# Expert layout of a two-layer diffusion trunk on one core: ten blocks with parts of 32, 64 or 128 slots, a seventh weight buffer, and a later start of the result gathers

## The chip, the core and the metric

The kernel runs on one core of one Trainium2 chip. The metric is the device time of one launch in microseconds; less is better. TensorE does the matrix products, VectorE and ScalarE copy and combine, GpSimd computes small scalars and issues the indexed transfers, and SyncE issues the weight transfers. All transfers run on the core's 16 DMA engines.

## The reference

One inference step of a trunk with two layers over 384 tokens (128 context, 256 latent) of width 1024. Each layer has a mixer (windowed attention beside a state-space scan) and then a mixture of 16 experts of which each token uses two. The mixture is what the change touches:

```
def moe_ffn(h, w_router, router_bias, w_gate_l, w_up_l, w_down_l):
    ...
    scores = jax.nn.sigmoid((t @ w_router).astype(jnp.float32))
    sel = scores + router_bias.astype(jnp.float32)
    grp = sel.reshape(-1, N_EXPERT_GROUPS, EXPERTS_PER_GROUP)
    grp_score = lax.top_k(grp, TOP_K)[0].sum(axis=-1)
    best = jnp.argmax(grp_score, axis=-1)
    ...
    _, idx = lax.top_k(masked, TOP_K)
    ...
    hid = jax.nn.silu(jnp.einsum('nd,edf->enf', t, w_gate_l)) * jnp.einsum('nd,edf->enf', t, w_up_l)
    hid = hid * gates.T[:, :, None].astype(hid.dtype)
    out = jnp.einsum('enf,efd->nd', hid, w_down_l)
```

Everything is float32. An expert has three matrices of 1 MB (gate, up: 1024 x 256; down: 256 x 1024), so a layer's experts are 48 MB of weights. Worked out from the reference's router on its inputs, the tokens of experts 0 to 15 are 38, 35, 30, 51, 43, 30, 42, 31, 99, 72, 105, 52, 45, 13, 45, 37 in layer 0 and 57, 50, 46, 37, 21, 24, 31, 26, 48, 76, 62, 38, 69, 49, 47, 87 in layer 1.

## The kernel before

The program is written by hand for the five engines, each with its own sequence and explicit waits on semaphores; no scheduler moves anything. The mixture of one layer runs so:

- Routing. TensorE makes router scores, VectorE chooses two experts a token, TensorE sums their positions. `FIXED` experts (0 and 1) have slots whatever their load. The other experts are ranked by their number of tokens; the ranking (`order`, L1442, signalled by `s_order`) tells SyncE which expert's weights to load next.
- Blocks. The work is cut into `NB` = 11 blocks of 128 slots. A block is a full expert (128 slots) or two experts of 64 slots: experts 0 and 1 and the ranks 0 to 3 have a block each, the ten lighter experts share five. For a block VectorE builds a one-hot selection (`fixed_one_hot`, `one_hots`), TensorE turns it into token numbers (`slot_tokens`, in four lists, `LISTS`), VectorE writes `idx`, and GpSimd gathers the token rows from `h_rows` (L711). TensorE transposes the rows (`rows`, L2218), multiplies by gate and up (`gate_up`, L2228, 8 steps), transposes the hidden values (L2235) and multiplies by down (`down`, L2244, 4 steps). Two 64-slot halves are products of 64 stationary columns each, issued in turn into the two halves of one bank. The sequence is `first_half(b+1)`, `hid_of(b)`, `rows(b+2)`, `second_half(b)`. `rows(1)` and the third list stand in the middle of `first_half(0)`.
- Results. ScalarE copies a block's result (`store`, L997) and, for the first `STORED` = 8 blocks, stores it in `y_exp` (L1002). The last three blocks (`LATE`) stay on chip and are added by products with a selection (`late_results`, L2290). For the stored ones GpSimd gathers, per token tile t of three, two result rows per token (L718, 0.5 MB each, six gathers) once the blocks' stores have landed; ScalarE scales the one (`weighted`, L1007), VectorE adds the other (L1550), then come gate and residual (`added`, `late_added`, `updated`) and the next layer's norm.
- Weights. SyncE loads units of 2 MB (gate and up of one expert, or down of a pair) into `ring`, six buffers (`SLOTS`). Each unit waits until its buffer's last holder has been used (`EARLIER`). Three mixture units (experts 0 and 1) can be loaded before the ranking is known, the others only after it. After the mixture of layer 0, SyncE waits for the last result gather (`combined`) before it loads the next layer's input weights.
- `clock_kept` is products that compute nothing and keep TensorE at work while it has to wait.

`xn` (3 x 1024 per partition) holds the normed tokens, then the accumulated results (`acc`); `xpad` (3072) holds the convolution input, then gates and gathered results (`first_y`).

## Time and profile before

| | us |
|---|---|
| median of 3 runs | 799.59 |
| lowest, highest | 797.41, 799.68 |
| profiled execution, whole | 799.34 |
| its span | 797.6 |
| TensorE busy in the span | 742.6 (93%) |
| VectorE, ScalarE, GpSimd busy | 329.5, 216.4, 142.0 |
| moved by DMA | 211.56 MB, mean 265 GB/s |

The span is the profiled execution without 1.7 us around it. In the trace the mixture of layer 0 lies between about 250 and 412 us, that of layer 1 between about 625 us and the end. TensorE's busy time counts overlapping products once. A row of a timeline names its idle time before it, and who ended it, in brackets.

### The profile page before, as it was taken

The numbers are of one execution on the slowest core, as the hardware profiler recorded it, in microseconds if no ns is written. First come the engines' busy times: TensorE is split into PE (matmuls) and PEld (weight loads), VectorE is DVE, ScalarE is ACT, GpSimd is POOL, SyncE is SP. The second block draws the span as 40 slices with busy tenths as digits, with TensorE's granted clock in tenths as the row PEclk, the third lists the DMA queues.
The fourth block names the chain that finished last, engine by engine and source line by source line (L and its number), as shares of the span: only waits on it lengthen the run. The fifth ranks groups of instructions, "written<-read, shape, count | busy, mean of one in ns | idle before, by whom it ended". The sixth has DMA issues, their size and how long they took to land. (4 is left out here: it accounts for less than half of the span.)

```text
span 797.6 us, 9586 instructions
## 1 busy us (share of the span) xinstructions
PE 742.6 (93%) x3528; PEld 372.2 (47%) x3528; DVE 329.5 (41%) x874; ACT 216.4 (27%) x492; POOL 142.0 (18%) x238
## 2 busy tenths in 40 slices
PE   3999997999999999999999999889999799999994
PEld 1456652455446444443344755345545544444331
DVE  2023534656436453212272262564643734331136
ACT  2210255724023110111312025683312301101121
POOL 4146041120011200000212404222000120000202
PEclk9999998999999999999999999999999999999998
DMA  8997225679422999999897233657420499999961
GB/s 323 387 341 252 95 107 211 219 283 400 181 74 114 390 392 409 424 424 422 315 389 246 83 106 112 212 176 295 190 106 1 158 409 357 418 424 421 424 241 79
DMA packets 66340, 211.56 MB, mean 265 GB/s; under 512 B 7883, under 2 KB 8755, under 8 KB 54003
## 3 DMA queue, kind: packets, MB, share of 16 engines
q1 hardware_dynamic: 52744, 179.33, 58.1%
q10 hardware_dynamic: 7851, 17.70, 5.8%
q0 software_dynamic: 5696, 13.89, 4.9%
q8 instruction: 29, 0.48, 0.2%
q14 instruction: 20, 0.16, 0.1%
HBM read 202.02 MB, written 13.93 MB: 271 GB/s over the span
## 5 line engine op out<-in xcount | busy, mean ns | idle before, releaser
L2228 PE MATMUL bank<-ring,work 128*64 128x512 f32 (+1 forms) x512 | 157.6, 598 | 3.0 <-DMA ring<-in_w_up_dram 2.5
L2228 PEld LDWEIGHTS bank<-ring,work 128*64 128x64 f32 (+1 forms) x512 | 59.1, 158 | 96.0 <-issue 94.4
L2244 PE MATMUL bank<-ring,xs_tok 128*64 128x512 f32 (+1 forms) x256 | 79.9, 597 | 2.0 <-DVE xs_tok L1573 1.0
L1573 DVE COPY xs_tok<-bank 128x256 f32<-128x256 f32 x22 | 9.3, 424 | 149.2 <-PE bank L2235 149.2
L1858 PE MATMUL bank<-hT,ring 128*128 128x384 f32 x192 | 62.2, 486 | 0.0
L1732 PE MATMUL bank<-ring,cpad 128*32 128x512 f32 x384 | 49.4, 636 | 6.6 <-DMA ring<-in_w_ada_dram 5.8
L1858 PEld LDWEIGHTS bank<-hT,ring 128*128 128x128 f32 x192 | 36.5, 190 | 25.0
L2244 PEld LDWEIGHTS bank<-ring,xs_tok 128*64 128x64 f32 (+1 forms) x256 | 28.3, 157 | 39.1 <-issue 35.0
L990 ACT ACTIVATE xs_tok<-bank 128x256 f32<-128x256 f32 x22 | 8.5, 385 | 139.7 <-PE bank L2228 139.7
L2116 PE MATMUL bank<-ring,xn 128*128 128x512 f32 x96 | 43.6, 597 | 0.0
L997 ACT ACTIVATE qkv<-bank 128x512 f32<-128x512 f32 x40 | 21.7, 595 | 79.4 <-PE bank L2244 79.4
L2116 PE MATMUL bank<-ring,xs_tok 128*128 128x512 f32 x96 | 43.2, 592 | 0.0
L1803 PE MATMUL bank<-ring,hT 128*128 128x512 f32 x96 | 42.8, 597 | 0.4 <-ACT hT L801 0.4
L1915 PE MATMUL bank<-ring,hT 128*128 128x512 f32 x96 | 42.3, 593 | 0.0
L711 POOL DMA_INDIRECT hT<-h_rows,idx x18 | 18.4, 1022 | 126.7 <-PE bank L2218 77.7
L1562 DVE COPY work<-bank 128x512 f32<-128x512 f32 x42 | 27.1, 686 | 11.6 <-PE bank L2218 11.6
L1170 DVE SCALAR_TENSOR_TENSOR conv<-xpad,prm,conv 128x388 f32<-128x388 f32 x48 | 29.9, 623 | 1.7
L2116 PEld LDWEIGHTS bank<-ring,xs_tok 128*128 128x128 f32 x96 | 18.2, 190 | 23.0 <-issue 23.0
L1803 PEld LDWEIGHTS bank<-ring,hT 128*128 128x128 f32 x96 | 17.7, 190 | 22.6 <-issue 20.4
L1915 PEld LDWEIGHTS bank<-ring,hT 128*128 128x128 f32 x96 | 17.8, 190 | 20.1 <-issue 20.1
L2116 PEld LDWEIGHTS bank<-ring,xn 128*128 128x128 f32 x96 | 17.4, 190 | 19.2 <-issue 19.2
L1732 PEld LDWEIGHTS bank<-ring,cpad 128*32 128x32 f32 x384 | 10.6, 113 | 29.1 <-issue 20.6
(392 smaller groups left out, 1057.2 us busy)
## 6 DMA issues: line engine op xcount, KB each, us to landing
ring<-in_w_ada_dram SPq DMA_DIRECT2D x48, 1024.0 KB, 8.8
ring<-in_w_gate_dram SPq DMA_DIRECT2D x32, 1024.0 KB, 13.1
ring<-in_w_up_dram SPq DMA_DIRECT2D x32, 1024.0 KB, 16.8
ring<-in_w_down_dram SPq DMA_DIRECT2D x32, 1024.0 KB, 14.6
ring<-in_w_in_dram SPq DMA_DIRECT2D x16, 1024.0 KB, 14.5
ring<-in_w_out_dram SPq DMA_DIRECT2D x8, 1024.0 KB, 7.3
y_exp<-qkv ACTq DMA_DIRECT2D x16, 512.0 KB, 8.4
xpad<-gate_rows ACTq DMA_DIRECT2D x6, 512.0 KB, 4.9
```

The costliest lines, as they stand in the source:

```text
L711: pool.indirect_dma_start(out=xg[b % 4], out_offset=None, in_=h_rows[:, :], in_offset=bass.IndirectOffsetOnAxis(ap=idx[:, b:b + 1], axis=0 ...
L997: act.activation(y_buf(e)[:, hf * 512:(hf + 1) * 512], bank[5 + hf][:, :], ACT.Copy).then_inc(s_yc, 1)
L1170: ins = dve.scalar_tensor_tensor(out=conv[:, m, :], in0=xpd[:, m, k:k + CONVW], scalar=tap(k), in1=conv[:, m, :], op0=ALU.mult, op1=ALU.add)
L1562: dve.tensor_copy(xgT[:, b, hf * 512:(hf + 1) * 512], bank[3 + hf][:, :]).then_inc(s_xgc, 1)
L1573: dve.tensor_copy(hidT[:, b, :], bank[2][:, 0:F]).then_inc(s_htc, 1)
L1732: last = mm(bank_of(i)[ADA_TILE * q:ADA_TILE * (q + 1), :], cpad[:, c:c + ADA_TILE], slot(ADA_AT[j])[:, kt, :], start=j == a and kt < ADA_ ...
L1803: last = mm(bank[t][:, :], tok(kt, t), slot(u[0])[:, kt, :], start=kt == 0, stop=kt == KT - 1)
L1858: last = mm(bank[(6 + m) % 8][:, 0:3 * P], slot(v)[:, kt, col:col + P], hT[:, kt, :], start=kt == 0, stop=kt == KT - 1)
L1915: last = mm(bank[4 + t][:, :], tok(kt, t), slot(u[3])[:, kt, :], start=kt == 0, stop=kt == KT - 1)
L2116: last = mm(bank[2 * t + hf][:, :], mixed[:, t, kt * P:(kt + 1) * P] if kt < 4 else xs_tok[:, t, (kt - 4) * P:(kt - 3) * P], slot(u + hf)[ ...
L2228: last = mm(bank[b][i * n:(i + 1) * n, :].rearrange("p (i f) -> p i f", i=2), rows_T[:, kt * P + i * n:kt * P + (i + 1) * n], gate_up_of(s ...
L2244: last = mm(bank[5 + hf][i * n:(i + 1) * n, :], hidT[:, b, f * P + i * n:f * P + (i + 1) * n], w[:, f, hf * 512:(hf + 1) * 512], start=f = ...
```

## The change

The layout has ten blocks instead of eleven:

- Experts 0, 1 and 2 are fixed, with 96 slots each. Of the 13 ranked ones, ranks 0 and 1 have 128 slots, ranks 2 and 3 have 96, ranks 4 to 11 have 64, and rank 12 has 32. Together these are 1280.
- A block holds parts of one width: one of 128, two of 64, or four of 32. An expert of 96 slots is three parts of 32, or one of 32 and one of 64 in another block. Three blocks a layer (0, 2 and 5) have four parts, five have two, two have one. Expert 2 lies in blocks 1 and 2, so its weights stay until block 2 has used them.
- `STORED` is 7; results are stored at rows of their expert, in one or two transfers a block, 12 a layer instead of 8 (of 3.7 MB instead of 4.2 MB).
- `xn` and `xpad` become one tensor, `arena`, and 4096 columns in it are a seventh buffer (`EXTRA`), which holds rank 0's and then another expert's gate and up. The results are gathered over the same columns.
- Four and a half units instead of three can be loaded before the ranking: gate and up of 0, 1 and 2, down of 0 and 1, down of 2.
- The second list of slots (block 1) moves behind the ranking on VectorE, and behind the other products on TensorE.
- GpSimd waits for the layer's last weight unit before it issues the six result gathers, and ScalarE scales all three tiles after its last `store`, not between the stores; VectorE adds tile 0 after the loop.
- The landing semaphores are counted over seven, and two semaphores for norm weights become one.
- VectorE computes the new capacities with six small operations more, in `combination`.

```
-FIXED = 2
+FIXED = 3
-SLOTS = 6
+SLOTS, EXTRA, LANDED = 6, 6, 7
...
+FULL, WIDE, NARROW = 2, 4, 12
+FIXED_CAP = 96
+cap_of = lambda r: CAP if r < FULL else HALF + CAP // 4 if r < WIDE else HALF if r < NARROW else CAP // 4
...
+quarters = lambda x, *at: tuple((x, Q * i, Q) for i in at)
+BLOCKS = [parts_of(*quarters(0, 0, 1, 2), *quarters(1, 0)),
+          parts_of((1, Q, HALF), (2, 0, HALF)),
+          parts_of(*quarters(2, 2), *quarters(3, 0, 1, 2)),
+          parts_of((4, 0, CAP)),
+          parts_of((5, 0, CAP)),
+          parts_of(*quarters(6, 0, 1, 2), *quarters(7, 0))] + [parts_of((x, 0, HALF), (x + 1, 0, HALF)) for x in (8, 10, 12, 14)]
...
+        extra = arena[:, DM:DM + UNIT]
...
-        LISTS = ((0, 1), (1, 2), (2, 7), (7, NB))
-        ROWS_AT = 5
+        LISTS = ((0, 1), (1, 2), (2, 6), (6, NB))
+        ROWS_AT = 4
...
+                    if EARLIER[u] is not None:
+                        sp.wait_ge(*used(EARLIER[u]))
+                    else:
+                        sp.wait_ge(s_h, 16 * NT * (l + 1))
+                        sp.wait_ge(s_x1, 2 * NT * (l + 1))
...
+                u = MOE_AT[l] + MOE_U - 1
+                pool.wait_ge(landed[u % LANDED], 32 * (u // LANDED + 1))
                 pool.wait_ge(s_yidx, l + 1)
...
-                    if e == NB - 2:
-                        act.wait_ge(s_yidx, l + 1)
-                        weighted(0)
-                    if e == NB - 1:
-                        weighted(1)
-                        weighted(2)
...
                     store(e, e % 2)
+                act.wait_ge(s_yidx, l + 1)
+                for t in range(NT):
+                    weighted(t)
...
                 lists(0)
-                lists(1)
-                clock_kept(4, 4)
+                clock_kept(4, 6)
                 if l == 0:
                     ada_columns(ADA_GAP)
-                clock_kept(4, 4)
+                clock_kept(4, 2)
+                lists(1)
...
-                        for i, s in enumerate(slots):
-                            last = mm(bank[b][i * n:(i + 1) * n, :].rearrange("p (i f) -> p i f", i=2),
-                                      rows_T[:, kt * P + i * n:kt * P + (i + 1) * n], gate_up_of(s)[:, kt, :, :],
+                        for s, at, n in parts:
+                            last = mm(bank[b][at:at + n, :].rearrange("p (i f) -> p i f", i=2),
+                                      rows_T[:, kt * P + at:kt * P + at + n], gate_up_of(s)[:, kt, :, :],
                                       start=kt == 0, stop=kt == KT - 1)
```

TensorE's sequence from the first list of layer 0 to block 1's first products. `tok_id` products are the lists (one bank each), `amask` products are `clock_kept`, `ident,hT` products transpose gathered rows, `ring,work` products are gate and up. Before:

```order
L1755 MATMUL bank4<-amask,ident 128x256 x2
L2195 MATMUL bank3<-tok_id,conv 128x2 x3
L2195 MATMUL bank0<-tok_id,conv 128x2 x3
L1755 MATMUL bank4<-amask,ident 128x256 x4
L1748 MATMUL bank5<-fold,qkv 128x4 x4
L1755 MATMUL bank4<-amask,ident 128x256 x4
L2218 MATMUL bank3<-ident,hT 128x128 x4
L2218 MATMUL bank4<-ident,hT 128x128 x4
L1755 MATMUL bank2<-amask,ident 128x256
L2228 MATMUL bank0<-ring,work 128x512 x4
L2218 MATMUL bank3<-ident,hT 128x128 x4
L2218 MATMUL bank4<-ident,hT 128x128 x4
```

And now:

```order
L2280 MATMUL bank3<-tok_id,conv 128x2 x3
L1840 MATMUL bank4<-amask,ident 128x256 x6
L1833 MATMUL bank5<-fold,qkv 128x4 x4
L1840 MATMUL bank4<-amask,ident 128x256 x2
L2280 MATMUL bank0<-tok_id,conv 128x2 x3
L2303 MATMUL bank3<-ident,hT 128x128 x4
L2303 MATMUL bank4<-ident,hT 128x128 x4
L1840 MATMUL bank2<-amask,ident 128x256
L2312 MATMUL bank0<-ring,work 32x512 x16
L2303 MATMUL bank3<-ident,hT 128x128 x4
L2303 MATMUL bank4<-ident,hT 128x128 x4
L2280 MATMUL bank2<-tok_id,conv 128x2 x12
```

The second list (bank0) now stands last before block 0's rows are transposed, and block 0's products are in sets of four with 32 columns each.

SyncE's weight issues around the wait for the ranking (`expert_order_made`) in layer 0. Before:

```order
L464 DMA ring<-in_w_down_dram 128x2048 [waits out_mm]
L464 DMA ring<-in_w_down_dram 128x2048
L514 TENSOR_LOAD qT [waits expert_order_made]
L514 ISA x2
L464 ISA [waits out_mm]
L464 DMA ring<-in_w_gate_dram 128x2048
L464 DMA ring<-in_w_up_dram 128x2048
L514 TENSOR_LOAD qT
L514 ISA x2
L464 ISA [waits ada_mm]
L464 DMA ring<-in_w_gate_dram 128x2048
L464 DMA ring<-in_w_up_dram 128x2048
```

And now:

```order
L533 DMA ring<-in_w_gate_dram 128x2048 [waits out_mm]
L533 DMA ring<-in_w_up_dram 128x2048
L533 DMA ring<-in_w_down_dram 128x2048 [waits out_mm]
L533 DMA ring<-in_w_down_dram 128x2048
L533 DMA ring<-in_w_down_dram 128x2048 [waits ada_mm]
L582 TENSOR_LOAD qT [waits expert_order_made]
L582 ISA x2
L533 ISA [waits ada_mm]
L533 DMA ring<-in_w_gate_dram 128x2048
L533 DMA ring<-in_w_up_dram 128x2048
L533 DMA ring<-in_w_down_dram 128x2048
L582 TENSOR_LOAD qT
```

The gate and up of expert 2 and one half of the split down unit now stand ahead of the wait, 3 MB more; behind it comes the other half (the row with one down issue), and next, not shown, the seventh buffer's unit.

GpSimd's gathers of rows (`h_rows`) and of results (`y_exp`) in layer 0. Before:

```order
L711 DMA hT<-h_rows,idx 128x1024 [waits xg_transposed,slot_tokens_made] x3
L711 DMA rot<-h_rows,idx 128x1024 [waits xg_transposed,slot_tokens_made]
L711 DMA hT<-h_rows,idx 128x1024 [waits xg_transposed,slot_tokens_made] x3
L718 DMA rot<-y_exp,y_idx 128x1024 [waits y_stored0,y_stored1,result_rows_made,xg_transposed]
L718 DMA xn<-y_exp,y_idx 128x1024
L718 DMA xpad<-y_exp,y_idx 128x1024
L718 DMA xn<-y_exp,y_idx 128x1024
L718 DMA xpad<-y_exp,y_idx 128x1024
```

And now:

```order
L792 DMA rot<-h_rows,idx 128x1024 [waits slot_tokens_made]
L792 DMA hT<-h_rows,idx 128x1024 [waits xg_transposed,slot_tokens_made] x3
L792 DMA rot<-h_rows,idx 128x1024 [waits xg_transposed,slot_tokens_made]
L792 DMA hT<-h_rows,idx 128x1024 [waits xg_transposed,slot_tokens_made] x2
L799 DMA rot<-y_exp,y_idx 128x1024 [waits y_stored0,result_rows_made,y_stored1,landed3,xg_transposed]
L799 DMA arena<-y_exp,y_idx 128x1024 x5
```

The first of them also waits for `landed3`, the semaphore of the last unit.

## Rows read from the trace of the kernel before

**Rows 1.** Stretches: start:end, length, busy us by engine (count), PEclk, DMA, GB/s.

```profile
320.00:360.00 40.00, 40.00 (x168) 17.32 (x166) 8.80 (x25) 4.58 (x10) 0.99 (x1) 1.00 1.01 423
600.00:640.00 40.00, 35.16 (x196) 22.14 (x195) 22.21 (x63) 11.69 (x27) 4.13 (x7) 0.96 0.26 100
720.00:760.00 40.00, 39.37 (x167) 16.16 (x167) 6.12 (x12) 4.41 (x9) 5.94 (x6) 1.00 1.01 422
```

**Rows 2.** TensorE timeline (start us, us, line, operands): expert blocks, `clock_kept` at 629.54.

```profile
284.14 7.09 PE L2228 MATMUL bank<-ring,work 128*64 128x512 f32 x32
...
295.74 7.03 PE L2228 MATMUL bank<-ring,work 128*128 128x512 f32 x16
...
379.89 7.09 PE L2228 MATMUL bank<-ring,work 128*64 128x512 f32 x32 [1.90 <-DMA ring<-in_w_up_dram]
...
629.54 3.70 PE L1755 MATMUL bank<-amask,ident 128*128 128x256 f32 x16
...
659.71 7.09 PE L2228 MATMUL bank<-ring,work 128*64 128x512 f32 x32
...
767.98 3.65 PE L2244 MATMUL bank<-ring,xs_tok 128*64 128x512 f32 x16 [0.94 <-DMA ring<-in_w_down_dram]
```

**Rows 3.** TensorE timeline: two sets of four 32-wide products, and what follows them.

```profile
20.88 1.92 PE L1732 MATMUL bank<-ring,cpad 128*32 128x512 f32 x16
22.73 0.70 PE L1755 MATMUL bank<-amask,ident 128*128 128x256 f32 x2
```

**Rows 4.** SyncE timeline, layer 0: issues before and after the ranking.

```profile
234.15 0.80 SPq L464 DMA_DIRECT2D ring<-in_w_down_dram  x2
259.17 0.36 SPq L464 DMA_DIRECT2D ring<-in_w_gate_dram  x1
```

**Rows 5.** TensorE timeline, layer 0: selection sums, row transposes, first products.

```profile
254.84 0.21 PE L2195 MATMUL bank<-tok_id,conv 128*128 128x2 bf16 x3
...
258.00 1.97 PE L1755 MATMUL bank<-amask,ident 128*128 128x256 f32 x8
261.05 1.06 PE L2218 MATMUL bank<-ident,hT 128*128 128x128 f32 x8 [1.08 <-DMA hT<-h_rows,idx]
...
262.97 3.70 PE L2228 MATMUL bank<-ring,work 128*128 128x512 f32 x8 [0.42 <-DVE work L1562]
266.82 1.09 PE L2218 MATMUL bank<-ident,hT 128*128 128x128 f32 x8 [0.15 <-DMA hT<-h_rows,idx]
```

**Rows 6.** GpSimd timeline, layer 0: gathers of token rows for blocks 0 and 1.

```profile
257.03 1.18 POOL L711 DMA_INDIRECT hT<-h_rows,idx  x1 [12.78 <-DVE idx L1412]
258.52 1.05 POOL L711 DMA_INDIRECT hT<-h_rows,idx  x1 [0.30 <-issue]
```

**Rows 7.** The chain that ended last, layer 1: start us, us, what.

```profile
632.59 10.37 DMA hT<-h_rows,idx
...
742.86 7.80 DMA y_exp<-qkv
...
757.98 14.36 DMA xn<-y_exp,y_idx
```

**Rows 8.** ScalarE, then TensorE timeline, end of layer 0.

```profile
395.31 1.15 ACT L1007 ACTIVATE xn<-xn,wt 128x1024 f32<-128x1024 f32 x1 [0.73 <-DMA xn<-y_exp,y_idx]
...
396.33 2.84 PE L2290 MATMUL bank<-qkv,conv 128*128 128x512 f32 x6
...
405.88 1.88 PE L2290 MATMUL bank<-qkv,conv 128*128 128x512 f32 x4
408.63 1.09 PE L1774 MATMUL bank<-ident,xn 128*128 128x128 f32 x8 [0.87 <-DVE xn L1118]
```

**Rows 9.** TensorE where its clock was low: timeline, then busy time by stretch.

```profile
637.80 4.74 PE L2228 MATMUL bank<-ring,work 128*128 128x512 f32 x8
...
136.00:139.00 3.00, 2.95 (x14) 0.96 (x18) 0.62 (x3) 3.00 (x11) 0.67 (x2) 0.50 0.02 7
790.00:797.00 7.00, 0.00 (x0) 0.00 (x0) 2.91 (x3) 1.15 (x2) 0.73 (x2) 0.51 0.39 156
```

257 lines of the change are left out of this document (152 added, 105 removed).

## The prediction

> **What bounds the kernel now.** I first read the busy time by stretch [rows 1]. TensorE has no gap to speak of, so that view alone would make a dropped block worth its whole time. But in the two stretches inside the mixtures the DMA engines are full as well, at 422 to 423 GB/s, while just before the mixture of layer 1 they are used to 26%. The TensorE timeline [rows 2] shows which of the two is behind: the last block waits 1.90 us for gate and up weights in layer 0, and in layer 1 the last down product waits until 767.98. Transfers and products end together. The chain of waits [rows 7] says what the end really follows: a block's result lands at 750.66, the six result gathers are issued, the last at 757.98, and they land at 772.34, far behind because weights flow beside them. In layer 0 the last one lands at 395.31 [rows 8]. So the bound of each mixture is the stream of weights and gathers, and the price of the change is what it does to the landing of the last result rows: 395.31 and 772.34.
>
> **One block fewer.** A block is 11.6 us of TensorE: one gate and up starts at 284.14, the next at 295.74 [rows 2]. That is off the path except where it frees buffers, and the transfers shrink by one row gather and half a megabyte of stores, 1 MB a layer, 2.5 us of stream.
>
> **Four parts a block.** Two sets of four 32-wide products take 22.73 - 20.88 = 1.85 us to the next product, 0.93 a set [rows 3]; a step of two 64-wide ones takes 0.88 (eight in 7.0 us, [rows 2]). So I take 0.05 a step, 12 steps a block, 0.6 us a block with four parts, and 1.8 us a layer for three. The bounds are 0 and 0.12 a step. The Trainium skill, "TensorE: Matmul & The Clock Gate", Part 3 on packing small matmuls, measured a speedup of 2.38, not 3, for three column tiles of 32; at that rate a set of four takes 1.1 us, and the sum below would be 6 us longer. The rows show four packing almost fully.
>
> **More weights ahead of the ranking.** Before, the last unit that needs no ranking is issued at 234.15 and the next at 259.17 [rows 4], in a time when the DMA engines are mostly idle. Now 3 MB more land there, worth 3.15 / 0.423 = 7.4 us of stream, in a time when no one waits. The seventh buffer takes 2 MB more right after the ranking. But the gain is not kept, because buffers then run out. The two gate and up units of block 5 get the buffers of experts 2 and 3, which come free only when block 2's gate and up is done, since expert 2 lies in blocks 1 and 2, and SyncE issues in order. By a count of the units in that order everything issued until then (4.2 MB behind block 0's and 1's gate and up) has landed some 5 us before. So the stream rests, restarts there, and is full to the end.
>
> **The second list moved back.** Before, block 1's rows are gathered from 258.52, right behind block 0's [rows 6], and TensorE transposes them at 266.82 after 0.15 us of waiting [rows 5]. Now their list stands behind all clock-keeping products, which end at 258.00 + 1.97 = 259.97 [rows 5]. From block 0's list at 254.84 [rows 5] to its gather at 257.03 [rows 6] were 2.2 us with ranking work between; without that I take 1.6 us, so the gather starts at about 261.3 (the list itself may be 0.3 earlier, since VectorE builds one selection before it, not two). That is 2.8 us later, and `first_half(0)` has `rows(1)` in its middle: TensorE stops there until 269.6. In layer 1 the gather before starts at 632.59 and takes 10.37 us [rows 7]; there the keeping products end at 629.54 + 3.70 = 633.24 [rows 2], and the gather starts 1.9 us later, so its rows land at 644.9. Bounds are 0 (the DMA engines give the late gather a larger share) and 5 us (it queues behind the weights issued first). Behind this wait stand lists 2 and 3 and all later gathers, so the whole block sequence shifts with it.
>
> **When block 2's gate and up ends.** Before, with `rows(1)` at 266.82, it ends at 291.1 [rows 2], 24.3 us later. Now 0.8 us of four-part steps come in and 0.4 us of a small row wait goes: 269.6 + 24.7 = 294.3. In layer 1: 643.0 to 666.7 [rows 2, 7] is 23.7; 644.9 + 24.5 = 669.4.
>
> **The stream after it.** 15 units of 2.097 MB, six stores and four row gathers of 0.524 MB are 36.7 MB. At 423 GB/s [rows 1] that is 86.8 us: the last weights land at 381.1 in layer 0. In layer 1, at 422, at 756.4, and 0.4 more for the final norm's weights, which ScalarE now loads beside it: 756.8. In layer 1 before it was 767.98.
>
> **The result gathers.** Before, the last of six is issued 757.98 - 750.66 = 7.3 us after its release [rows 7]. Now it is released by the last weights. Alone, a gather takes 261.05 - 257.03 = 4.0 us from issue to use [rows 5, 6], not 14.36. So the last result rows land 11.3 us after the last weights: 392.4 and 768.1, that is 2.9 and 4.2 us earlier than before. The Trainium skill, "DMA: Bandwidth & Descriptors", fits a transfer issued by GpSimd as 2.0 us plus its bytes at 436 GB/s; that would be 3.2 us, and 0.8 us a layer better. On GpSimd nothing is queued behind the new wait but the norm. SyncE waits for the gathers before it loads the next layer's input weights; these have 15 us until they are needed at about 410.
>
> **Behind the gathers.** TensorE's last block ends, before, at 396.33 [rows 8]. Now: -11.6 -1.9 (the weight wait) +2.8 +1.8 = 387.4. ScalarE's copies and three scalings follow, and the third has to wait for 392.4 anyway: moving `weighted` behind the stores costs nothing unless the rows come before 390. The late products, 11.4 us without a wait (396.33 to 407.76), are over at 398.9. The next layer's transposes, before at 408.63, hang on VectorE's chain and come at 405.7. So TensorE stands still for 6.8 us where it stood 0.87. What the clock does after such a rest: in the last 7 us, without a product, it is granted at 0.51, the 1.2 GHz level [rows 9]. Back at work it stays there for a while: eight products took 4.74 us instead of 3.70, a loss of 1.0 [rows 9, 5], and in 136 to 139 the clock is 0.50 with TensorE busy all the time, a loss of 1.5 in that stretch alone. TensorE is the bound from the transposes on, so this counts. I take 2.1, between 1.0 and twice 1.5. In layer 1 nothing follows that needs the clock.
>
> **The six small VectorE operations** and the extra store issues lie beside products; VectorE is busy 8.8 of 40 us there [rows 1]. Without that cover they would be some 1 us a layer.
>
> **Sum.** -2.9 (layer 0) + 2.1 (clock) - 4.2 (layer 1) = -5.0 us. 799.34 - 5.0 = 794.3; the median shown is 0.25 above the profiled execution, so I forecast **794.5**. Its own range is 791 to 798.
>
> **Rivals.**
>
> *The stream does not rest.* If block 1's rows come without the delay, or the early 3 MB carry through, the last weights land by 376 and 751, and TensorE sets the end: its last block at 387.4, in layer 1 at 762.8 (771.6 - 11.6 - 0.9 + 1.9 + 1.8), then 1.1 us of copies and three scalings of 1.15. The last scaling starts at 390.8 and 766.2: 4.5 and 6.1 us gained, 2.1 given back, 791. For it: 7.4 us of prefetch. Against it: the buffers. 17%.
>
> *Parts of 32 do not pack.* A set of four takes 0.93 us if all run at once and 2 x 0.88 if two do. At 1.1, 20 sets before block 2's gate and up is done cost 0.17 each more, 3.4 us a layer, and the time is 801, within 0.3% of before. Against it: [rows 3]. The skill's figure above is this case. 6%.
>
> *The stop in `first_half(0)` becomes the bound, slower.* TensorE stops there in a place where it already rested for the first rows. If block 1's gather takes 2 us more than before, and the clock falls in the stop, as it did in layer 1 (4.74 for 3.70), another 2.1 us, every later buffer is freed 4 us later, and so are the last weights: 8.4 us in all, 802.7. It decides from the point where block 2's gate and up ends 2.9 us after 294.3 in layer 0 and 4.2 us after 669.4 in layer 1; from there nothing is gained. For it: DMA is full from 259, and the early issues stand ahead of that gather. Against it: before, the same gather shared the engines with as many weights. 14%.
>
> *The layout does not hold the tokens.* Then an overflow round runs all 16 experts again, 50 MB or 119 us of stream at 423 GB/s: over 900 us. Loads by rank are 105, 99, 72, 52, 51, ... 13 and 87, 76, 69, 62, 49, ... 21, against 128, 128, 96, 96, 64, ... 32; fixed ones at most 57 of 96. Excluded but for an error: 1%.
>
> **How the numbers follow.** The forecast has 55%. Small mixtures around no change have 7%. A measurement of this kernel tells 0.3%, 2.4 us, from no change. Faster: 51 of the forecast's 55 and the 17 of the first rival, 68%. Within: 4, the 6, the 7 and 2 of the slower rival, 19%. Slower: 13%. The range goes from 3 below the first rival to the middle between the second and the third: 788 to 801.5; about 1 in 10 lies outside on either side.
>
> **What would show it.** Right: the transposes of block 1's rows wait 2 to 3 us; DMA falls for some 5 us before block 2's gate and up ends, and is full from then on; the last down weights land near 381 and (shifted by layer 0) 756; the last result gather needs about 4 us; TensorE rests 5 to 8 us before the next layer's transposes and runs at half clock after it. Wrong: TensorE's blocks waiting for weights from block 3 on (stream slower than taken), or the last scaling following ScalarE's copies at once (the first rival), or four-part blocks over 8 us of gate and up.

## The result: slower, and the profile of the changed kernel

The changed kernel takes 806.68 us (median of 20 runs), the kernel before 799.92 in the same comparison. The ratio is 1.0074, with a 95% interval of 1.0058 to 1.0090: 0.74% slower. Two of the 20 executions, of 969.52 and 1262.68 us at granted clocks of 0.75 and 0.56, are slow ones that the ratio leaves out. Forecast were 794.5, with a range of 788 to 801.5. The profiled execution has a span of 806.8 us where it was 797.6.

Five marks that both programs have show where the 9.2 us came from.

| | before | after | step after | difference of the step |
|---|---|---|---|---|
| layer 0: last down product ends | 396.40 | 398.55 | | +2.15 |
| first transposes of the next norm | 408.63 | 415.76 | 12.23, now 17.21 | +4.98 |
| layer 1: routing sums begin | 627.61 | 637.73 | 218.98, now 221.97 | +2.99 |
| last down product ends | 771.63 | 778.18 | 144.02, now 140.45 | -3.57 |
| end of the span | 797.6 | 806.8 | 25.97, now 28.62 | +2.65 |

Only one step is shorter. With one block of 11.6 us fewer, the mixture of layer 0 still ends 2.15 us later, and what follows each mixture is longer.

**The head of layer 0.** The row transposes of block 0, which stood at 261.05 with 1.08 us of waiting [rows 5], in TensorE's timeline of the changed kernel:

```profile
266.68 1.94 PE L2303 MATMUL bank<-ident,hT 128*128 128x128 f32 x8 [6.62 <-DMA hT<-h_rows,idx]
...
291.31 7.05 PE L2312 MATMUL bank<-ring,work 128*32 128x512 f32 x64
```

The gather they wait for, in GpSimd's timeline, and the first weights behind the ranking in SyncE's:

```profile
257.94 1.29 POOL L792 DMA_INDIRECT hT<-h_rows,idx  x1 [13.26 <-DMA h_rows<-arena]
```

```profile
258.64 0.35 SPq L533 DMA_DIRECT2D ring<-in_w_gate_dram  x1
```

Before, the gather was issued at 257.03, as soon as its list was there [rows 6], 2.1 us ahead of the first weights at 259.17 [rows 4]. Now it waits for something else, the landing of the last `h_rows` store, and starts at 257.94, 0.9 us later, while the first weights go 0.5 us earlier, at 258.64. The lead is down to 0.7 us. Its rows come 8.7 us after the issue instead of 4.0.

Stretches of the same kernel (start:end, length, busy us by engine and count, PEclk, DMA, GB/s):

```profile
245.00:250.00 5.00, 4.07 (x58) 2.76 (x51) 3.72 (x12) 2.68 (x8) 0.00 (x0) 1.00 1.00 362
250.00:255.00 5.00, 4.55 (x42) 2.60 (x40) 4.18 (x18) 2.79 (x6) 0.00 (x0) 1.00 0.95 384
260.00:265.00 5.00, 0.05 (x3) 0.00 (x0) 2.02 (x6) 0.00 (x0) 1.01 (x1) 0.66 0.95 382
265.00:270.00 5.00, 3.33 (x14) 2.31 (x18) 1.28 (x3) 1.33 (x2) 0.00 (x0) 0.50 1.02 424
275.00:280.00 5.00, 5.00 (x53) 1.77 (x53) 4.12 (x17) 0.00 (x0) 2.67 (x3) 1.00 0.28 66
295.00:300.00 5.00, 5.00 (x44) 2.06 (x38) 2.96 (x15) 0.38 (x1) 0.00 (x0) 1.00 0.64 212
```

In the first two stretches the DMA engines are full with the weights loaded ahead of the ranking; the `h_rows` stores, issued at 246.5, 251.4 and 252.9, go through the same engines. Before, the DMA share there was 0.27 and 0.53. From 260 to 265 TensorE does next to nothing (0.05 us), and its granted clock falls to 0.66 and then to 0.50, the 1.2 GHz level: the transposes take 1.94 us instead of 1.06. Then comes what the forecast had named, a pause of the stream: 66 GB/s from 275 to 280 and 212 from 295 to 300, since buffers come free late.

**The tail of layer 0.** TensorE, GpSimd, ScalarE (with its last scaling of layer 1) and VectorE, from the last block on:

```profile
363.59 7.09 PE L2312 MATMUL bank<-ring,work 128*64 128x512 f32 x32 [1.14 <-DMA ring<-in_w_up_dram]
...
379.70 9.44 PE L2312 MATMUL bank<-ring,work 128*64 128x512 f32 x32 [4.20 <-DMA ring<-in_w_up_dram]
...
394.90 3.65 PE L2327 MATMUL bank<-ring,xs_tok 128*64 128x512 f32 x16
...
415.76 1.97 PE L1859 MATMUL bank<-ident,arena 128*128 128x128 f32 x8 [5.85 <-DVE arena L1199]
```

```profile
390.26 0.99 POOL L799 DMA_INDIRECT rot<-y_exp,y_idx  x1 [65.37 <-DMA ring<-in_w_down_dram]
...
396.75 0.99 POOL L799 DMA_INDIRECT arena<-y_exp,y_idx  x1 [0.30 <-issue]
```

```profile
398.88 1.08 ACT L1080 ACTIVATE work<-bank 128x512 f32<-128x512 f32 x2 [4.08 <-PE bank L2327]
399.85 3.22 ACT L1091 ACTIVATE arena<-arena,wt 128x1024 f32<-128x1024 f32 x3
```

```profile
781.56 1.15 ACT L1091 ACTIVATE arena<-arena,wt 128x1024 f32<-128x1024 f32 x1 [0.18 <-DMA arena<-y_exp,y_idx]
```

```profile
401.03 1.29 DVE L1636 SCALAR_TENSOR_TENSOR arena<-rot,wt,arena 128x1024 f32<-128x1024 f32 x1 [6.53 <-ACT arena L1091]
402.36 2.61 DVE L1636 SCALAR_TENSOR_TENSOR arena<-arena,wt 128x1024 f32<-128x1024 f32 x2
405.00 1.22 DVE L1641 TENSOR_TENSOR arena<-arena,conv 128x1024 f32<-128x1024 f32 x1
```

The last block waits 4.20 us for gate and up weights, and its eight steps take 9.44 us where they took 7.09 [rows 2]. The last down product starts at 394.90, the copies at 398.88, and the three scalings follow without a wait. The result rows, gathered from 390.26 on, are there at 401.65, where SyncE, which waits for them, issues again; the third scaling starts at about 402.0. So two things end together behind the last block: TensorE with ScalarE's copies and scalings, and the rows, which waited for the last weights. In layer 1 it is the rows: the third scaling, at 781.56 (shown among the rows above), waits 0.18 us for them. VectorE begins the last addition of its chain (L1641) at 405.00, 6.5 us after the end of TensorE's last down product (394.90 + 3.65); before it did so (L1555) at 397.87, 1.5 us after it. These are the 5.0 us of the table. TensorE then stands still for 5.85 us, and its clock is low again.

The end of the stream, the same columns as above:

```profile
384.00:386.00 2.00, 2.00 (x12) 0.77 (x10) 0.00 (x0) 0.00 (x0) 0.00 (x0) 0.88 1.01 422
386.00:388.00 2.00, 2.00 (x12) 0.73 (x10) 0.00 (x0) 0.00 (x0) 0.00 (x0) 1.00 0.37 152
388.00:390.00 2.00, 1.50 (x8) 0.35 (x4) 0.46 (x2) 0.39 (x1) 0.00 (x0) 1.00 0.04 16
390.00:396.00 6.00, 5.98 (x26) 2.11 (x28) 0.71 (x2) 1.09 (x2) 4.52 (x5) 1.00 0.55 160
396.00:402.00 6.00, 6.00 (x20) 2.32 (x17) 0.97 (x1) 3.12 (x5) 1.44 (x2) 1.00 0.62 213
```

The weights flow at 422 GB/s until 386.3, and the last of them lands near 389: two and a half us with 0.3 MB in them. The gathers, which wait for it, then have the DMA engines alone and move 160 and 213 GB/s.

### The profile page after: what moved, and what is told of

Same layout as the page of the kernel before. It is cut to its first block and busy times, and to the rows that moved or that the text cites. A ratio compares the mean times of both kernels' runs of the same rounds, so it can differ in the third digit from the quotient of the medians.

```text
span 806.8 us, 10286 instructions
## 1 busy us (share of the span) xinstructions
PE 730.4 (91%) x3886; PEld 356.5 (44%) x3886; DVE 325.0 (40%) x882; ACT 213.1 (26%) x486; POOL 141.4 (18%) x234
## 5 line engine op out<-in xcount | busy, mean ns | idle before, releaser
L2312 PE MATMUL bank<-ring,work 128*32 128x512 f32 (+2 forms) x704 | 134.1, 619 | 10.3 <-DMA ring<-in_w_up_dram 9.9
L2312 PEld LDWEIGHTS bank<-ring,work 128*32 128x32 f32 (+2 forms) x704 | 42.1, 129 | 97.0 <-issue 95.4
L2327 PE MATMUL bank<-ring,xs_tok 128*32 128x512 f32 (+2 forms) x384 | 73.0, 597 | 1.0 <-DVE xs_tok L1659 1.0
L2201 PE MATMUL bank<-ring,arena 128*128 128x512 f32 x96 | 43.6, 597 | 0.0
L1080 ACT ACTIVATE qkv<-bank 128x512 f32<-128x512 f32 x36 | 19.5, 595 | 79.3 <-PE bank L2327 79.3
L2327 PEld LDWEIGHTS bank<-ring,xs_tok 128*32 128x32 f32 (+2 forms) x384 | 22.4, 127 | 38.4 <-issue 35.3
L1648 DVE COPY work<-bank 128x512 f32<-128x512 f32 x38 | 24.6, 686 | 15.0 <-PE bank L2303 15.0
L1251 DVE SCALAR_TENSOR_TENSOR conv<-arena,prm,conv 128x388 f32<-128x388 f32 x48 | 29.9, 623 | 1.7
L2303 PE MATMUL bank<-ident,hT 128*128 128x128 f32 x128 | 18.3, 291 | 11.9 <-DMA hT<-h_rows,idx 11.9
L2312 PE MATMUL bank<-arena,work 128*128 128x512 f32 (+1 forms) x64 | 28.4, 597 | 0.0
```

The costliest lines, as they stand in the source:

```text
L1080: act.activation(y_buf(e)[:, hf * 512:(hf + 1) * 512], bank[5 + hf][:, :], ACT.Copy).then_inc(s_yc, 1)
L1251: ins = dve.scalar_tensor_tensor(out=conv[:, m, :], in0=xpd[:, m, k:k + CONVW], scalar=tap(k), in1=conv[:, m, :], op0=ALU.mult, op1=ALU.add)
L1648: dve.tensor_copy(xgT[:, b, hf * 512:(hf + 1) * 512], bank[3 + hf][:, :]).then_inc(s_xgc, 1)
L2201: last = mm(bank[2 * t + hf][:, :], mixed[:, t, kt * P:(kt + 1) * P] if kt < 4 else xs_tok[:, t, (kt - 4) * P:(kt - 3) * P], slot(u + hf)[ ...
L2303: last = tr(bank[3 + kt // 4][:, kt % 4 * P:(kt % 4 + 1) * P], buf[:, kt * P:(kt + 1) * P], ident[:, :])
L2312: last = mm(bank[b][at:at + n, :].rearrange("p (i f) -> p i f", i=2), rows_T[:, kt * P + at:kt * P + at + n], gate_up_of(s)[:, kt, :, :], ...
```

## Experiments

My theory after this reading had two parts. **The head**: weights issued behind the ranking overtake block 0's rows. **The tail**: the scalings stand behind the last store and lengthen the chain behind the last block. The rivals: the amount of the stream decides whatever is done at either end, or the new wait of GpSimd is the loss. All ratios are against the kernel before, run on the same chip; the x, y and z runs were on three chips, so runs of different letters are compared by their ratios.

| kernel | what differs | median us | ratio | 95% interval |
|---|---|---|---|---|
| changed kernel |  | 806.68 | 1.0074 | 1.0058 to 1.0090 |
| x1_rows0 | SyncE waits for block 0's rows | 798.25 | 0.9964 | 0.9942 to 0.9986 |
| x2_rows01 | and for block 1's | 800.24 | 0.9994 | 0.9978 to 1.0010 |
| x3_list1 | second list as before | 798.37 | 0.9981 | 0.9960 to 1.0001 |
| x4_nolast | no wait for the last weights | 809.29 | 1.0080 | 1.0051 to 1.0109 |
| y1_results | that, and the scalings as before | 795.21 | 0.9907 | 0.9875 to 0.9939 |
| y2_layout | that, and the second list as before | 789.07 | 0.9842 | 0.9805 to 0.9878 |
| y3_before_late | kernel before, scalings behind, last-weights wait | 813.49 | 1.0155 | 1.0129 to 1.0180 |
| z4_before_behind | kernel before, scalings behind | 813.13 | 1.0149 | 1.0128 to 1.0171 |
| y4_keep | y2_layout, 16 keeping products | 790.07 | 0.9857 | 0.9834 to 0.9881 |
| z1_ordered | y2_layout, SyncE waits for block 0's rows | 786.47 | 0.9827 | 0.9807 to 0.9847 |
| z2_ordered_keep | z1_ordered, 16 keeping products | 789.54 | 0.9851 | 0.9829 to 0.9872 |
| z3_six | z1_ordered, no seventh buffer | 795.21 | 0.9926 | 0.9905 to 0.9948 |

### The head: the gather alone (x1_rows0, x2_rows01)

```
                     if (pair, k) == (SPLIT[0], 1):
                         sp.wait_ge(s_order, l + 1)
+                        sp.wait_ge(gathered[0], 16 * (uses(BUFS, 0) * l + 1))
```

The second run has the same line for `gathered[1]` as well.

> The changed kernel, but SyncE waits, behind the ranking, until block 0's token rows have landed before it issues further weights. Theory 'the head': in the changed kernel the first rows land at 266.7 (261.05 before) because weights issued at 258.6 flow beside their gather; alone it needs 4 us, so rows(0) comes at about 262.3 in layer 0, the clock does not fall to 0.50, the first products take 3.7 and not 4.8 us, and block 2's gate and up ends at 293 to 295 instead of 298.3. Since the stream rests until then, the later issue of the weights costs nothing, and the last weights land 3 to 4 us earlier a layer: 799 to 802 us against 806.7. Rival 'the stream': the amount of weights behind sets the end, the later issue only delays it; the last weights stay at 389 or come later, 806 to 809 us.

> As the run with SyncE waiting for block 0's rows, but it waits for block 1's rows too. Theory 'the head': block 1's gather is alone as well and takes 4 us instead of 8 to 10; in layer 0 it was in time behind the late first rows, in layer 1 TensorE waited 2.90 us for it. So rows(1) comes at about 266 in layer 0, and block 2's gate and up ends at about 292; weights that block 2 needs at 285 are issued at about 266, in time. 797 to 801 us. If the weights behind the ranking are needed sooner than that, TensorE waits for them in block 2 and the time is that of the changed kernel, 805 to 808 us.

The first run is 1.1% faster than the changed kernel by the ratios, 8.8 us, a little more than expected: the head's theory holds and the rival falls. TensorE's row transposes in it, and the last block:

```profile
262.86 1.94 PE L2304 MATMUL bank<-ident,hT 128*128 128x128 f32 x8 [1.75 <-DMA hT<-h_rows,idx]
...
373.91 9.39 PE L2313 MATMUL bank<-ring,work 128*64 128x512 f32 x32 [4.20 <-DMA ring<-in_w_up_dram]
```

The rows come 4.0 us after the issue at 258.87, as before the change, and the last block starts 5.8 us earlier. It still waits 4.20 us for weights, so the stream bounds it in this run too; what moved is the whole sequence. The line acts in both layers. By the marks of the table above, 5.8 of the 10.5 us between the two profiled executions come in the mixture of layer 0 and 4.5 in that of layer 1. There block 0's rows had hardly been late (4.6 us after their issue, here 4.2). Block 1's had: TensorE waited 2.90 us for them in the changed kernel, and here it does not wait at all. Their gather is now issued ahead of the weights (638.23 against 639.70) and not behind them (644.24 against 642.24).

The second run's time lies in its range, but it gains nothing on the first, and block 1's rows come at 270.57, not at 266. They had not been late in layer 0, and SyncE now issues its first weights 2.0 us later (265.8 instead of 263.8). The last block starts 2.3 us later, at 376.2. Of these, 1.2 us are not the weights': block 0's first products, whose weights were loaded long before, took 5.02 us in this execution where they took 3.76 in the first run. The intervals of the two ratios overlap a little, so what the later issue itself costs is not shown; that it is worth something to wait for the second gather too is not shown either.

### The list's place (x3_list1)

On VectorE `one_hots(0, LISTS[1][1])` builds both selections first, and `slot_tokens(1)` and `lists(1)` stand where they stood before the change.

```
                 lists(0)
+                lists(1)
                 clock_kept(4, 6)
...
                 clock_kept(4, 2)
-                lists(1)
```

> The changed kernel with the second list of slots where it was before: ahead of the ranking on VectorE and right behind the first list on TensorE. Theory 'the head': SyncE's issues come about 0.5 us later as before, both gathers are issued at about 258 and 259.5 and share the engines with the weights; the first rows still land late (263 to 266), so at most 1 to 2 us a layer come back: 803 to 806 us. Rival 'the list': the later list is the whole loss, and the time falls to 799 or below.

The rival's number came, 798.4, not mine. But not by the rival's mechanism:

```profile
257.20 1.23 POOL L792 DMA_INDIRECT hT<-h_rows,idx  x1 [13.01 <-DVE idx L1493]
258.73 1.01 POOL L792 DMA_INDIRECT hT<-h_rows,idx  x1 [0.30 <-issue]
```

```profile
258.94 0.35 SPq L533 DMA_DIRECT2D ring<-in_w_gate_dram  x1
```

```profile
261.45 1.06 PE L2302 MATMUL bank<-ident,hT 128*128 128x128 f32 x8 [1.40 <-DMA hT<-h_rows,idx]
...
267.38 1.09 PE L2302 MATMUL bank<-ident,hT 128*128 128x128 f32 x8 [0.38 <-DMA hT<-h_rows,idx]
```

Block 0's gather is issued 1.7 us ahead of the weights, and its rows land in time, at 261.45, with 1.40 us of waiting. The list's place moved the weights 0.3 us back, and in this execution the gather was free to go when its list was there, 0.7 us earlier; that was enough. The list of block 1 itself was never late in layer 0. In layer 1 it was: by the marks this execution is 8.3 us ahead of the changed kernel's at the end of layer 0's mixture and gains another 4.1 in that of layer 1, where block 1's rows are there in time (642.58, no wait). That a shift of some tenths decides was the question of a later run (z1_ordered).

### The wait for the last weights (x4_nolast), and the results as before (y1_results)

```
-                u = MOE_AT[l] + MOE_U - 1
-                pool.wait_ge(landed[u % LANDED], 32 * (u // LANDED + 1))
                 pool.wait_ge(s_yidx, l + 1)
```

> The changed kernel without GpSimd's wait for the last weights: the six result gathers are issued once the stored blocks have landed, at about 370, and flow beside the last weights. If the wait costs (the gathers, 3.15 MB or 7.4 us of stream, end 12.3 us behind the last weights, at 401.65, and the last scaling with them), the rows are there when the last block's copies are done at 400 and 1 to 2 us a layer come back, unless the last weights land up to 7.4 us later. If the wait gains, as its place says, the last block waits for its weights up to 7 us longer (4.2 us now) and the time rises to 809 to 815 us. I expect slightly slower, 807 to 812.

y1_results has this and ScalarE's and VectorE's old order too:

```
+                    if e == NB - 2:
+                        act.wait_ge(s_yidx, l + 1)
+                        weighted(0)
+                    if e == NB - 1:
+                        weighted(1)
+                        weighted(2)
...
                     store(e, e % 2)
-                act.wait_ge(s_yidx, l + 1)
-                for t in range(NT):
-                    weighted(t)
```

> The changed kernel with its part on the results undone: no wait for the last weights on GpSimd, and the three scalings between the last stores. Theory 'the tail': from the last down product's end to the next layer's transposes are 17.3 us in the changed kernel (398.5 to 415.8) and 12.3 before (396.4 to 408.6); to the end of the span they are 28.6 and 26.0, because three scalings and VectorE's first additions stand behind the last copies. Without the last-weights wait alone nothing came back (809.3 against 806.7), since the scalings still stood there. Undone together they give 5.0 + 2.6 = 7.6 us: 799 to 802 us. Rival 'only the head and the weights count': the time stays at 805 to 809.

Without the wait the ratio is 1.0080, with it 1.0074: as long as the scalings stand behind the last store, the wait of GpSimd neither costs nor gains. The gathers issued at 372.1 delay the last block's weights by little (it starts at 379.05, with 4.82 us of waiting), and the rows are there by 393.87, 7.8 us sooner than with the wait, for scalings that start at 398.27.

With the wait gone, the order of the scalings (and of VectorE's first addition) does cost: x4_nolast and y1_results differ in nothing else, and lie 1.7% apart.

The other single edit, the old order with the wait kept, was not run. From the rows of the changed kernel my estimate is that it would give back 1 us at most: from the landing of the last rows (401.65, 781.56) to VectorE's L1641 (405.00, 784.34) are 3.35 and 2.78 us, where the kernel before has 2.56 and 2.55 (395.31 to 397.87, 772.37 to 774.92). So by the rows either part is enough to hold the chain back, and only undoing both frees it.

The profiled spans of x4_nolast and y1_results are 807.3 and 793.5. By the marks of the table above, the 13.8 us are 2.7 up to the last down product of layer 0 (block 0's rows came that much earlier in this execution of y1_results), 5.6 from there to the next transposes (16.92 and 11.29), 1.4 to the routing of layer 1, -0.2 in its mixture and 4.2 behind it (28.6 and 24.4). So the scalings' place costs 11.2 us here. I had expected 799 to 802 us from the two edits, a gain of 7.6; the median is 795.21, since with the rows in time both chains get shorter than they were in the kernel before.

### The same two edits on the kernel before (y3_before_late, z4_before_behind)

Both put the scalings behind the last store of the kernel before; y3_before_late also adds the wait for the last weights.

> The kernel before with the change's part on the results alone: GpSimd waits for the layer's last weights, and the scalings stand behind the last store. Forecast of the blind sum: the gathers land 11 to 12 us behind the last weights. Before, those flow beside the gathers until about 390 and 767; without them the last weights come up to 7.4 us (3.15 MB) sooner, about 384 and 760. Theory 'the tail': the last scaling then follows at about 400 (396.4 + 1.0 + 3.2) instead of 396.5 and the next transposes at 413 instead of 408.6: 2 to 4 us a layer lost, 803 to 808 us. Rival 'the earlier weights pay for it': 797 to 801.

> The kernel before with the three scalings behind the last store (and VectorE's first addition behind the loop), but no wait for the last weights. It splits the 12 us that both together cost the kernel before (813.5 against 801.6). From the traces: scalings behind the last copies put 5.0 us between the last down product and the next transposes of layer 0 and 2.6 us behind layer 1, and the clock falls in that rest (1 to 2 us): 808 to 811 us. What is left to 813.5 is the wait's: rows that land at 402.2 and 786.3 where the copies end at 398 and 781.5. If the wait were the whole, the time would stay at 801 to 803.

1.0155 with both, 1.0149 with the scalings alone: on this kernel too the order of three ScalarE instructions (with VectorE's first addition) is enough for the whole loss, 12 us, and the wait adds nothing that can be measured on top. Both expectations were too small, the first by 5 us and the second by 2. The rival of the first (earlier weights pay) fell: the last weights land at about 390 without the gathers beside them. That does not clear the wait. In y3_before_late ScalarE does wait for the late rows, in both layers:

```profile
402.19 1.15 ACT L1009 ACTIVATE xn<-xn,wt 128x1024 f32<-128x1024 f32 x1 [0.82 <-DMA xn<-y_exp,y_idx]
...
786.33 1.15 ACT L1009 ACTIVATE xn<-xn,wt 128x1024 f32<-128x1024 f32 x1 [1.37 <-DMA xn<-y_exp,y_idx]
```

By the marks, its steps behind the two last blocks are 1.7 and 2.1 us longer than those of z4_before_behind, and the mixtures ahead of them 1.4 and 2.4 us shorter. The wait alone on this kernel was not run. ScalarE, VectorE and TensorE of z4_before_behind:

```profile
399.32 3.22 ACT L1007 ACTIVATE xn<-xn,wt 128x1024 f32<-128x1024 f32 x3
```

```profile
400.51 1.28 DVE L1547 SCALAR_TENSOR_TENSOR xn<-rot,wt,xn 128x1024 f32<-128x1024 f32 x1 [6.25 <-ACT xn L1007]
```

```profile
380.11 8.78 PE L2224 MATMUL bank<-ring,work 128*64 128x512 f32 x32 [2.13 <-DMA ring<-in_w_up_dram]
...
415.24 1.97 PE L1770 MATMUL bank<-ident,xn 128*128 128x128 f32 x8 [5.57 <-DVE xn L1115]
417.00 3.62 PE L2286 MATMUL bank<-qkv,conv 128*128 128x512 f32 x4
```

By the marks of the table above, its 13.8 us over the span before are: 1.9 up to the last down product (394.66 + 3.65), 4.7 to the next transposes, 2.9 to the routing of layer 1 (637.12), 1.4 to the last down product of layer 1 (782.56), 2.9 to the end. The middle 2.9 (from the transposes to the routing) need not be the scalings': against the kernel before, the same step is 0.0 to 3.9 us longer in the profiled executions of y1_results, y2_layout, y4_keep and z1_ordered, where the scalings stand as before. Besides the chain itself, two places pay for the clock. Behind 5.57 us of rest the transposes take 1.97 us instead of 1.09, and four products 3.62 us instead of 1.88 [rows 8]. And the last gate and up take 8.78 us behind a wait of 2.13 us; before, they took 7.09 behind one of 1.90 [rows 2]. That second one no edit of this run explains, and in y3_before_late the same products kept 7.09 us behind a wait of 2.59 us in layer 1; I count it as chance of the execution.

### What is left is the layout (y2_layout), and its spread (z1_ordered)

y2_layout is y1_results with the second list as in x3_list1. So of the change there remain the ten blocks, the weights ahead of the ranking and the seventh buffer. z1_ordered adds SyncE's wait of x1_rows0.

> The changed kernel with both other parts undone: the result gathers and scalings as before, and the second list ahead of the ranking. What is left is the layout of ten blocks, the earlier weights and the seventh buffer. Theory 'head and tail': the losses add up, 8.3 us for the list's place (measured 798.4 against 806.7) and 7.6 for the results: 790 to 793 us, so the layout itself gains 7 to 9 us against the kernel before. Rival 'the stream': with the head and the tail mended, the last weights set the end and only one of the two comes back: 797 to 800.

> The layout alone (result gathers, scalings and second list as before), and SyncE waits behind the ranking until block 0's token rows have landed. Theory 'two orders': in the run of the layout alone the executions lay between 785.4 and 796.2; the profiled one, 796.2, had its first rows at 267.3, while with the same head another one had them at 261.5. So the order in which the gather and the weights reach the engines decides, and the wait settles it: 784 to 789 us with a spread of 5 us at most. Rival 'noise from elsewhere': the same median, 788 to 791, and the same spread of 10 us, and if the later issue of the weights costs, 791 to 794.

y2_layout: ratio 0.9842. The losses add up: 0.93% for the head (1.0074 to 0.9981) and 1.67% for the results (1.0074 to 0.9907) would give 0.9814. So what is left gains 1.6%, 12.5 us, more than I had expected of it.

Its six runs lie between 785.4 and 796.2. The profiled one was the slowest:

```profile
258.07 1.57 POOL L792 DMA_INDIRECT hT<-h_rows,idx  x1 [13.83 <-DMA h_rows<-arena]
```

```profile
258.99 0.35 SPq L533 DMA_DIRECT2D ring<-in_w_gate_dram  x1
```

```profile
267.33 1.94 PE L2304 MATMUL bank<-ident,hT 128*128 128x128 f32 x8 [7.24 <-DMA hT<-h_rows,idx]
```

The same program text as in x3_list1 at this place, but here the gather starts 0.9 us later, behind the store, its issue (258.07 + 1.57) ends behind the first weights' (258.99), and the rows come 9.3 us after its start instead of 4.3. With SyncE's wait the order is fixed, and the five runs lie between 785.5 and 788.7, median 786.47. The ratios, 0.9842 and 0.9827, can't be told apart. That the order is the cause of the spread is not shown: y4_keep below, without the wait, has six runs within 2.1 us, and x1_rows0, with it, twelve within 8.1. What the rows show is the lead and the landing in single executions (table in the last section). The rows come at 262.15, and the weights are issued when they have landed:

```profile
262.15 1.07 PE L2305 MATMUL bank<-ident,hT 128*128 128x128 f32 x8 [1.68 <-DMA hT<-h_rows,idx]
...
374.03 8.56 PE L2314 MATMUL bank<-ring,work 128*64 128x512 f32 x32 [5.36 <-DMA ring<-in_w_up_dram]
```

This kernel has the lowest ratio of the study, 1.7% under the kernel before and 2.5% under the changed one.

### The seventh buffer (z3_six)

`in_extra`, the function that says which units go to the seventh buffer, returns `False`; else as z1_ordered.

> As the layout alone with SyncE's wait for block 0's rows, but without the seventh buffer: rank 0's gate and up wait for a buffer of the ring like all others. The blind forecast said the stream rests for some 5 us before block 2's gate and up ends, whatever is loaded earlier, and starts again there. One buffer less is 2.1 MB more behind that point, 5.0 us of stream at 423 GB/s a layer: the last block waits up to 5 us longer, 792 to 797 us. Rival 'the early weights don't pay': block 2 ends when it did and the time is within 2 us of the run with seven.

0.9926 against 0.9827: the buffer is worth 1.0%, 8.7 us by the medians, 4.4 a layer, where 5.0 were expected. That is more than half of the 1.7% by which z1_ordered is under the kernel before. The forecast's idea of the stream (what is not loaded when block 2's gate and up ends is paid at 423 GB/s) has the right size. That the stream rests first is only in part so here: in z3_six DMA moves 358 GB/s from 264 to 280 and 366 from 280 to 290, in z1_ordered 401 and 410. The rival falls.

### Keeping the clock in the last wait (y4_keep, z2_ordered_keep)

```
                     pe.wait_ge(s_xgc, 2 * b + (2 * NB * l + 2))
+                    if b == NB - 1:
+                        clock_kept(4, 16)
```

> The layout alone (as the run with both other parts undone) plus 16 products without a use before the last block's gate and up, where TensorE waits about 4 us for its weights and the eight steps behind it then take 8.8 to 9.4 us at a granted clock of 0.55 to 0.88 instead of 7.09. Theory: the products take the place of the wait, the clock stays at the 2.4 GHz level and 1.5 to 2.3 us a layer come back: 3 to 4 us below that run. Rival: the end of the last block is not what the next step waits for (the result rows are), and the time is the same within 1 us.

> As the layout alone with SyncE's wait for block 0's rows, plus 16 products without a use before the last block's gate and up. In the earlier run with these products the last block took 7.09 us instead of 8.5 to 9.7, with its first product not later (374.9 from a block 2 that ended at 291.5: 83.4 us; without them 376.3 from 295.0: 81.3), so they take about 2 us and give back 2: the same as without them within 1.5 us, 784 to 789. If the clock is worth more than they cost: 2 to 3 us less.

The last gate and up of z2_ordered_keep take 7.09 us again, but start later:

```profile
371.55 7.17 PE L1842 MATMUL bank<-amask,ident 128*128 128x256 f32 x32
378.65 7.09 PE L2314 MATMUL bank<-ring,work 128*64 128x512 f32 x32
...
391.51 3.65 PE L2329 MATMUL bank<-ring,xs_tok 128*64 128x512 f32 x16
```

In z1_ordered (rows above) they take 8.56 from 374.03, and the last down product starts at 388.37, 3.1 us before this one. Of these, 2.9 are there before the added products: 1.0 from the head, and 2.0 because the block ahead of the last waits 2.84 us for weights instead of 0.87, which no edit of this run explains. The products themselves take 7.17 us where z1_ordered waited 5.36, and the eight steps behind them give 1.5 back. The first expectation fails and its rival's number comes; the second expectation (the same within 1.5 us, 784 to 789) is missed by half a us. The ratios are 0.9857 and 0.9842 in the one pair, 0.9851 and 0.9827 in the other; the intervals overlap, and no gain shows in either. Sixteen products are longer than the wait. Fewer were not tried.

## Why the prediction was wrong

**One block fewer, four parts a block.** Eight steps of four 32-wide parts take 7.05 us (291.31 above), eight of two parts 7.09. So the term of 1.8 us a layer is 0. The Trainium skill's figure in "TensorE: Matmul & The Clock Gate", Part 3 (2.38 times for three column tiles of 32), carried over to four as the prediction did, would give 1.1 us a step. This case, which has no set of three, shows 0.88 for four: they pack fully.

**The weights ahead of the ranking.** That the stream rests and starts again at the end of block 2's gate and up was right, and z3_six gives the size. The step put these weights "in a time when no one waits", with the DMA engines "mostly idle". But the `h_rows` stores use the engines there (0.53 of them before, from 250 to 255), and behind the stores waits block 0's gather, which is issued 0.9 us later. This is the first step that failed.

**The second list.** I had the delay at block 1's rows: at 269.6 instead of 266.8 in layer 0, with a wait of 2 to 3 us. In layer 0 they did not wait at all; block 0's rows did, 6.62 us. In layer 1 the step held:

```profile
645.41 1.06 PE L2303 MATMUL bank<-ident,hT 128*128 128x128 f32 x8 [2.41 <-DMA hT<-h_rows,idx]
...
653.87 1.77 PE L2303 MATMUL bank<-ident,hT 128*128 128x128 f32 x8 [2.90 <-DMA hT<-h_rows,idx]
```

653.87, less the 10.1 us by which the layer starts later, is 643.8 (forecast 644.9), and block 2's gate and up ends at 679.5, less 10.1 is 669.4, as forecast. Its price there shows in x1_rows0 and x3_list1, where block 1's rows are in time and the mixture of layer 1 is 4.5 and 4.1 us shorter. In layer 0 it ends at 298.4, 4.1 us behind the forecast.

**The stream after it.** 36.7 MB at 423 GB/s, 86.8 us. Measured are some 90.6 (298.4 to 389.0). The rate in the middle was right (423 GB/s from 310 to 386); both ends were not in the sum. The stream needs 2 us to begin (88 GB/s from 298 to 300) and 2.5 for the last part at 152 and 16 GB/s. The last weights land 7.9 us behind the forecast: 4.1 from block 2, 3.8 from this term.

**The result gathers.** 11.3 us were forecast from their release to their landing; measured are 11.4 (390.26 to 401.65, where SyncE, which waits for them, issues again). From the last weights' end near 389 to the release lies 1.3 us more, which the sum did not have. The last gather takes 4.9 us from its issue, where the sum had 4.0.

**When the last result rows land.** This is the term that decided, and it was mis-sized. The sum took it at 392.4 in layer 0; they land at 401.65, 9.3 us later: 4.1 from block 2, 3.8 from the stream's ends, 1.3 from the last weights to the release, 0.1 from the gathers. From there to the next transposes 14.1 us pass where 13.3 were forecast, because VectorE's three additions now stand in a row. In layer 1 the rows land at 781.56, less 10.1 is 771.4, where the sum had 768.1. From there to the end it is 25.2 us, as before. With 0.9 more for the clock these are 9.3 + 0.8 + 0.9 + 3.3 = 14.3, of the 14.2 by which the span missed.

**Behind the gathers.** TensorE's last block was to end at 387.4 and ended at 398.5. I had taken its 1.90 us of weight waiting off the sum, though the weights of the last block come with the same stream: it and the block ahead waited 1.14 + 4.20 us instead of none (5.3), the sequence started from a block 2 that was 4.1 later, and the last gate and up lost 2.4 to the clock. Less 0.6 for the four-part block behind block 2, that is 11.2, of 11.1 missed. So TensorE and the rows are late by about the same, and they still end together. "Moving `weighted` behind the stores costs nothing unless the rows come before 390" holds as it stands, with the wait kept: the rows come after the last copy, and the order adds 0.8 us in layer 0 and 0.2 in layer 1. What it hides is that only the wait makes it so cheap. In x4_nolast the rows are there 7.8 us sooner, and then the order of the scalings is what holds the chain. Against y1_results that is 11.2 us for both layers, on the kernel before 10.5 by the marks (4.7 + 2.9 + 2.9, the middle one not surely its own) or 12.3 by the medians. The sum priced the wait and the new order as rows that land 2.9 and 4.2 us sooner than in the kernel before. Set against the new layout with the old order and no wait, which I never worked out, the two together cost 11.6 us in the steps behind the mixtures (13.4 by the ratios of the changed kernel and y1_results).

**The clock behind the rest.** Forecast 6.8 us of rest and 2.1 us of loss; measured 5.85 and, from the transposes to the routing, 3.0, not all of which need be this (see the last section).

**The sum** of the steps measured in the table is +9.2 us; the forecast's was -5.0.

**The rivals.** "The stop in `first_half(0)`" (802.7, 14%) had the kind of mechanism, a late row gather with a fall of the clock, and the threshold (block 2's gate and up 2.9 us late in layer 0; it was 4.1). But in layer 0 the stop was at `rows(0)`, one gather earlier; only in layer 1 was it where the rival had it. By x1_rows0 the two are 9 of the 20 us between the changed kernel and z1_ordered. The other 11 were in no rival. "The stream does not rest" described what the kernel does once both are mended: in z1_ordered DMA moves 401 and 410 GB/s from 264 to 290. I gave the right bound the wrong price at either end.

**Open.** That a wait of the stores on the prefetched weights is the cause of the late gather was read from the traces; a run without the early weights but with seven buffers was not made. Nor was either part of the tail put back alone: the wait with the old order of the scalings, on either kernel.

## What to carry to other kernels

When two engines issue transfers within a microsecond of each other and one of them is small and urgent, don't leave the order to chance: make the bulk queue wait for the small one, if its stream has anything to spare, and look at where the small one lands in more than one execution. Before moving short instructions behind the last result, ask what ends last in the new schedule, not in the old one: here the same work ran under a product or behind it, 11 us apart over two layers. When two edits delay two inputs of the same step, undoing one shows nothing; a null result clears neither. And in a sum for a stream add its start and its last stragglers to bytes over rate.

## What the runs showed of the hardware

- What a small gather pays beside a full stream hangs on tenths of a microsecond. For block 0's gather of 0.5 MB in layer 0, by the issue's lead over the first of 5 MB of weights, in the profiled executions:

| lead, us | 0.5 (x4) | 0.7 (changed) | 0.9 (y2) | 1.3 (y1) | 1.7 (y4, x3) | 2.1 (before) | over 4 (x1, z3) |
|---|---|---|---|---|---|---|---|
| issue to use, us | 9.6 | 8.7 | 9.3 | 7.0 | 4.1, 4.3 | 4.0 | 4.0, 4.2 |

  The Trainium skill says in "DMA: Bandwidth & Descriptors", Queues, rings and completion order, that each DMA engine goes round robin between the queues it has work for, a packet at a time. At half of 423 GB/s the 0.5 MB would take 1.2 us longer; the rows with a lead under 1 us show 4.7 to 5.6, so in bytes the gather got far less than an even share. What a packet of either queue holds no run shows.
- A full stream of 422 GB/s ends with some 2.5 us in which 0.3 MB trickle in. A wait for "the last" transfer pays for them. A wait for an earlier unit was not tried.
- The same piece of attention in layer 1, behind the same wait of 1.06 us, ran at the 2.4 GHz level in the one profile and in part at 1.2 GHz in the other. TensorE before, and after the change:

```profile
514.88 0.50 PE L1948 MATMUL bank<-ident,xn 128*128 128x128 f32 x2 [1.06 <-DVE qkv L1238]
...
516.08 1.56 PE L1932 MATMUL bank<-work,qT 64*128 64x384 f32 x8
```

```profile
523.38 0.50 PE L2033 MATMUL bank<-ident,arena 128*128 128x128 f32 x2 [1.06 <-DVE qkv L1319]
...
524.69 2.93 PE L2017 MATMUL bank<-work,qT 64*128 64x384 f32 x8
```

The eight products take 2.93 instead of 1.56 us. Nothing in the change touches this place, and in the 10 us ahead of it TensorE's rows agree in length and waits to 0.01 us. It is one execution each, so it may account for a microsecond or two of the 3.0 us of the table in either direction.
